# A two-layer hybrid encoder step on one core: the order of the two token halves in the dense products

## What is computed

```python
# token_mix: three attentions A, B, C on the same xn
(a_q, a_k, ..., c_v, c_f) = split(xn @ w_in)          # combined input projection
o_a, o_b, o_c = dsa(...), stick_breaking(...), fox(...)
branch = einsum('btnw,nwd->btnd', stack([o_a, o_b, o_c]), w_branch)
gate = sigmoid(xn @ w_gate)                           # three gates of 1024 channels
x = x + (gate * branch).sum(branches) @ w_out
# conv_ffn, D_FF = 2816
h = xn @ w_up                                         # 2 x 2816 channels
hc = causal_conv3(h);  g, u = split(hc)
x = x + (silu(g) * u) @ w_down
```

## Time and profile before

| | us |
|---|---|
| median of three runs | 2085.11 |
| the three runs | 2084.97, 2085.11, 2086.62 |
| the profiled execution | 2086.56 |
| its span in the trace | 2084.8 |
| TensorE busy | 2071.7 |
| VectorE busy | 1390.1 |
| ScalarE busy | 1005.8 |
| GpSimd busy | 234.9 |

### The profile page before, as it was taken

How to read it: one execution, slowest core, us unless ns; L and a number is a source line. 1 busy time by engine, 2 the same in 40 slices (tenths; PEclk the granted TensorE clock), 3 DMA queues, 4 the chain that set the end, 5 groups by cost and what they waited for, 6 DMA issues and landing times.

```text
span 2084.8 us, 39646 instructions
## 1 busy us (share of the span) xinstructions
PE 2071.7 (99%) x15860; PEld 1969.0 (94%) x15860; DVE 1390.1 (67%) x2606; ACT 1005.8 (48%) x1635; POOL 234.9 (11%) x174
## 2 busy tenths in 40 slices
PE   9999999999999999999999999999999999999998
PEld 8888989998999999999998989899989999999998
DVE  7658786788737763676465786777787477536653
ACT  6267315647527652444352672265565366424433
POOL 0023000000040110011300220000001311001112
PEclk9999999999999999999999999999999999999999
DMA  6231323121222222222232212221212222232222
GB/s 205 79 107 41 92 83 106 52 72 52 61 89 82 82 89 94 81 82 90 91 111 81 96 42 92 81 98 61 72 52 72 71 91 81 90 92 84 87 88 92
DMA packets 54344, 175.21 MB, mean 84 GB/s; under 512 B 7076, under 2 KB 11860, under 8 KB 54212
## 3 DMA queue, kind: packets, MB, share of 16 engines
q1 hardware_dynamic: 47364, 158.88, 24.6%
q0 software_dynamic: 3072, 10.11, 1.2%
q10 hardware_dynamic: 3776, 4.34, 0.6%
HBM read 160.25 MB, written 12.90 MB: 83 GB/s over the span
## 4 chain that ended last, share of the span: by engine, by line
PE 96%; DVE 2%; ACT 1%; issue 0%; DMA 0%; SPq 0%; DVEq 0%
PE d L1522 63%; PE d L1576 14%; PE ab L1622 4%; PE d L1914 2%; PE d L1587 2%; PE d L1923 2%; PE ab L1863 1%; PE ab L1851 1%; PE d L1626 1%; PE ab L1900 1%; PE ab L1522 1%; PE ab L1677 0%; PE d L1768 0%; PE ab L1708 0%; PE ab L1718 0%; DVE w L900 0%
## 5 line engine op out<-in xcount | busy, mean ns | idle before, releaser
L489 ACT ACTIVATE wh<-raw 128x512 fp32r<-128x512 f32 x548 | 345.0, 631 | 715.8 <-PE d L1522 556.9
L861 DVE TENSOR_TENSOR wl<-raw,wh 128x512 fp32r<-128x512 f32 x548 | 389.8, 713 | 282.3 <-ACT wh L489 273.7
L1522 PE MATMUL d<-xh,wh 128*128 128x288 f32 x2400 | 511.7, 294 | 2.1 <-DVE xl L874 1.1
L1522 PE MATMUL d<-xl,wh 128*128 128x288 f32 x2400 | 509.1, 293 | 0.0
L1522 PE MATMUL d<-xh,wl 128*128 128x288 f32 x2400 | 509.0, 293 | 0.0
L1522 PEld LDWEIGHTS d<-xh,wh 128*128 128x128 f32 x2400 | 381.3, 188 | 7.7 <-issue 5.7
L1522 PEld LDWEIGHTS d<-xl,wh 128*128 128x128 f32 x2400 | 381.4, 188 | 0.0
L1522 PEld LDWEIGHTS d<-xh,wl 128*128 128x128 f32 x2400 | 381.4, 188 | 0.0
L1576 PE MATMUL d<-xh,wh 128*128 128x288 f32 x768 | 173.8, 308 | 0.0
L1576 PE MATMUL d<-xh,wl 128*128 128x288 f32 x768 | 164.8, 296 | 0.0
L1576 PE MATMUL d<-xl,wh 128*128 128x288 f32 x768 | 164.5, 295 | 0.0
(11 more groups left out here) (325 smaller groups left out, 3264.5 us busy)
## 6 DMA issues: line engine op xcount, KB each, us to landing
raw<-in_w SPq DMA_DIRECT2D x286, 512.0 KB, 3.5
out_o_k<-k POOLq DMA_DIRECT2D x4, 1152.0 KB, 7.2
out_o_v<-v POOLq DMA_DIRECT2D x4, 1024.0 KB, 8.9
x<-in_xT SPq DMA_DIRECT2D x8, 288.0 KB, 5.7
k<-in_bc_k_past ACTq DMA_DIRECT2D x4, 512.0 KB, 4.4
v<-in_bc_v_past ACTq DMA_DIRECT2D x4, 512.0 KB, 5.4
out_y<-z SPq DMA_DIRECT2D x4, 432.0 KB, 2.7
raw<-in_w SPq DMA_DIRECT2D x4, 256.0 KB, 6.0
```

What stands on the lines that cost most here:

```text
L489: act.activation(wh[:, c % SPLIT_SLOTS, :], stored, ACT.Copy).then_inc(high_done, 1)
L861: dve.tensor_tensor(lows, stored, highs, ALU.subtract).then_inc(low_done, 1)
L1522: ins = pe.matmul(outs[half], w_, r_[:, kk, HALF * half:HALF * half + HALF], start=first and n == 0 and begin, stop=last and n == len(kks) ...
```

## The change

`dense` and `gate_blocks` number their pairs of products (three for each weight block), and the parity of the number sets which half goes first: in even pairs the first half and then the second, in odd pairs the second and then the first. A new function `halves` gives the order. Before, it was the first and then the second in every pair. What is multiplied, the accumulators, the number of products, the waits and the counts are as they were; in `branch_first`, `by_token` and `down_half` nothing changes.

```diff
+            def halves(n):
+
+                return (n % 2, 1 - n % 2)
+
             def dense(before, lo_wait, c0, outs, rh, rl, kks, begin=True, end=True, behind=no_wait):
...
-                    for w_, r_, first, last in ((hi_w, rh, True, False), (hi_w, rl, False, False), (lo_w, rh, False, True)):
-                        for half in range(2):
+                    for i, (w_, r_, first, last) in enumerate(((hi_w, rh, True, False), (hi_w, rl, False, False), (lo_w, rh, False, True))):
+                        for half in halves(3 * n + i):
                             ins = pe.matmul(outs[half], w_, r_[:, kk, HALF * half:HALF * half + HALF],
                                             start=first and n == 0 and begin, stop=last and n == len(kks) - 1 and end)
...
# in gate_blocks
-                    for w_, r_, first, last in ((hi_w, xh, True, False), (hi_w, xl, False, False), (lo_w, xh, False, True)):
-                        for half in range(2):
+                    for i, (w_, r_, first, last) in enumerate(((hi_w, xh, True, False), (hi_w, xl, False, False), (lo_w, xh, False, True))):
+                        for half in halves(3 * kk + i):
                             ins = pe.matmul(dhalf[d][half], w_, r_[:, kk, HALF * half:HALF * half + HALF],
                                             start=first and kk == 0, stop=last and kk == KD - 1)
```

## The result

The changed kernel takes 2124.05 us (median of four runs, 2123.72 to 2124.87) against 2085.18 for the kernel before. The ratio is 1.0183, with a 95% interval of 1.0171 to 1.0195: slower by 1.8%, where 0.5% was forecast and 2112 us was the end of the range. The sign was right, the size was not, and the reason was not either.

The account below looks back on a forecast made before the run. TensorE, busy 99% of the span, was taken to bound the kernel. The profiled 2086.56 us plus 10.1 us for stays gave 2096.7, so a median of about 2095 us, 0.5% slower; range 2068 to 2112.

Parts of the forecast that it names:

- The sign: Whole kernel: the change was forecast to make it slower, by 0.5%, with chance 0.48 for slower against 0.30 for faster.
- What bounds the kernel: TensorE, busy 99% of a span of 2084.8 us; each nanosecond on a dense product reaches the end 1:1.
- The price of a stay: At borders of pairs, a product writing the same bank as the one ahead costs 2.7 ns more than one changing bank.
- the rival of no difference: Dense products: the bank is no matter, and changing weights or the one half slowed `down_half`; 2081 to 2089 us, chance 0.22.
- Adding it up: Stretches running at 130: 3760 of the 5916 stays at 2.7 ns each, +10.1 us; the other stretches add nothing.
- keeps the one that it starts with: Dense stretches: one order has two rates, 130 and some 133 ns a product, and a stretch holds its starting rate.
- Slower by more: Rival: all dense products fall to the slow rate, 2112 us; slower up to that rate, 2102 to 2115, chance 0.15.
- The bound: Upper end: all fast stretches, 7950 products, go to the slow rate at 3.45 ns each, +27 us, giving 2112 us.
- "Faster": Rival: changing bank costs the slow stretches' 3 ns, and half the changes go; 2068 to 2081 us 0.20, 2026 to 2068 0.10.
- the price of 122.5 ns: Skill's estimate for a warm 288-column product; if stays alone reached it, -44 us; noted beside the sum, not used in it.
- cycling through PSUM banks: Skill's rule for dense stretches: it leaves micro-idles that make the clock throttle; would favour faster, but added nothing to its chance.

## Why the prediction was wrong

- **What bounds the kernel: right.** All of the loss is time of TensorE, and it reached the end nearly 1:1: 37.5 us of span for 38.8 of busy time. ScalarE waited 602.1 us on the products instead of 556.9, and nothing new waits.
- **The price of a stay: the step that failed.** I took it from `down_half`, as 2.7 ns for each product that stays in its bank. The length of the row stands (it is 6.77 us for 51 again in the changed kernel, as nothing in it changed), but two things were mixed up in it. `down_half` stays in its bank *and* streams one half at a time (33 products of the first and then 18 of the second in this piece, so its 132.7 is a mean of two rates), and I gave the whole price to the bank. With the bank alone, the loss is nil (ratio 1.0002); with one half alone and the banks alternating, all the stretches that were fast go to 133.3 to 133.5. I had written down the doubt (the weights, "or the one half") and put it with the rival of no difference, where it led to the wrong end.
- **Adding it up: the second failure, and it made the size.** A price for each stay, 3760 x 2.7 = 10.1 us, supposes that the other products go on at 130. But 130 was met only in streams that alternate strictly, as a pace of the whole stretch and not as a price of a product. The changed order leaves no stretch in it: over the pieces that I counted as fast the loss is 3.9 ns for every product, 8.3 for every stay, three times the term. That a stretch "keeps the one that it starts with" stood in the prediction, and the conclusion was not drawn: an order that breaks the alternation could lose all of the fast pace at once. That case was there as a rival ("Slower by more", 2112 us), with a row that fits, the first half of `down_half` falling to the slow spacing at once; it was held down by the count of the stays, which is not what is paid for.
- **The bound.** 2112 supposed that nothing is slower than the slow rate, 133.5, and that the slow stretches pay nothing. Both are wrong by a little. The changed order runs at 133.3 to 134.5, so the pieces that I had counted as fast lost 31.1 us and not 27. Another 6.4 of the 37.5 us lie outside them: 2.5 in the two stretches of 288 products behind branch C, which took 37.49 us before, 130.2 each, were missing from my count of the fast ones, and take 38.72 after; 2.5 in the gate products (24 of them 3.25 us in the earlier trace rows, and 3.28 after); and the rest in small amounts. The medians differ by 1.4 us more than the two spans. Together that is the distance from 2112 to 2124.
- **The rivals.** "No difference" was right on the bank, by its rows, and wrong on the change, since the change is not only about the bank. "Faster" rested on a cost of changing the bank, and none can be measured: one bank for nearly all products gained 2.1 us in a single run, and 1.4 of it are layer 1's 336 products behind branch B and the 96 after them, which entered at the fast pace in that run (43.73 and 12.48 us in the rows above; 44.84 and 12.78 in the earlier trace rows). As a stretch behind B took either pace in two runs of one program, this gain can't be put down to the bank.
- **Of the Trainium skill:** the price of 122.5 ns ("TensorE: Matmul & The Clock Gate", section "Back-to-back issue gap", which gives its formula for an isolated product) was met by no long stretch in any kernel, the fastest being 130.0. What the skill tells of cycling through PSUM banks (same page, section "A second HAM failure mode: psum-queue depth-cycling") had nothing to act on: the granted clock is 1.00 in the slow stretches as in the fast.

**What stays open.** What the pace is in the machine. Shown is that it sits in the streaming of the tokens, that it is entered and kept, that places of start shift the rate by 1.7 ns, and that neither the bank, nor the half with which the weights change, nor contiguous reads, nor the tile decide it. Whether the changed order could be kept fast by some entry was tried with eight, and none was; that is no proof. Why it runs at 134.2 in the first up products and at 133.3 in the later ones is open. So is why a first half ahead of the pairs flips the stretches behind C and A and not those behind B and the first up products; for B one run says little, since the plain order too enters there at either pace.

## What to carry to other kernels

When a change alters two things at one border, here the bank that is written and the data that is streamed, price them apart before adding up; the nearest row of the trace may have both in it. Where the same code runs at two steady rates, ask what holds the faster one, since a change that breaks this loses it everywhere and not only at the places that it touches. A product that computes nothing may be there to hold it: taking one such product out of each layer cost 19 us.

## What the runs showed of the hardware

- A strictly alternating stream of products of 288 columns, and of 320 and 256, has two steady rates, 260 and 267 ns a pair, at the same granted clock. It keeps the one that it enters with, for up to 3168 products; a short product ahead, or its absence, can decide which (130.0 with it, 133.3 without).
- The entry need not be the same each time: 336 products of one and the same program took 43.73 us in one execution and 44.84 in another.
- The PSUM bank order doesn't move the time measurably: with a stay at every border of pairs the ratio is 1.0002 (interval 0.9992 to 1.0011), and with nearly all products of a call in one bank the long piece has the same 411.89 us, in one run.
- The start of the streamed columns within a row matters: products of 288 columns that all start at token 0, 8, 16, 64, 128, 144 or 256 take 133.3 ns, those at 32 or 288 take 131.6.
- No order that was tried ran a long stretch under 130.0 ns, and no version here beats the kernel before by more than a measurement can tell.
